# The SSM matrix C loaded and multiplied later in a two-layer decoder kernel, and a first scale with norm weight and bias inside its sums

## What is computed

```python
cs = silu(c)
mod = cs @ ada_w[i] + ada_b[i]                  # 2048 x 12288 per layer
sh1, sc1, g1, sh2, sc2, g2 = split(mod, 6)
h = rms_norm(x, norm1_g[i]) * (1.0 + sc1) + sh1  # the "first scale" is norm1_g * (1 + sc1)
...
# S5: discretisation, per group and state
step = exp(log_step); mag = exp(lr * step); ang = li * step
lb = mag * (cos(ang) + i sin(ang))               # its powers make tables
coef = (lb - 1) / (lr + i li)
bb = coef * b                                    # used here as b, with coef moved into C
y = Re(C x_t)
```

## Time and profile before

| | |
|---|---|
| median of 3 runs | 2718.32 us (2717.66 to 2719.12) |
| the profiled execution, its own time | 2721.41 us |
| its span in the trace | 2719.6 us |
| PE busy | 2653.0 us, 98% |
| VectorE (DVE) busy | 2276.5 us, 84% |
| ScalarE (ACT) busy | 1293.0 us, 48% |
| GpSimd (POOL) busy | 512.4 us, 19% |
| HBM read and written | 701.66 MB and 25.44 MB |

### The profile page before, as it was taken

One profiled execution on the slowest core, in us unless ns is written; L12 is line 12 of the kernel. 1 busy time (PEld: TensorE's weight loads), 2 busy tenths in 40 slices (PEclk: granted clock), 3 DMA queues, 4 the chain that ended last, 5 costly groups with the idle time before them and its releaser, 6 DMA issues.

```text
span 2719.6 us, 50038 instructions
## 1 busy us (share of the span) xinstructions
PE 2653.0 (98%) x18416; PEld 2377.3 (87%) x18416; DVE 2276.5 (84%) x3379; ACT 1293.0 (48%) x1869; POOL 512.4 (19%) x468
## 2 busy tenths in 40 slices
PE   5999999999999999999999999999999999999998
PEld 1998888888898888888888999999888888888887
DVE  6978988888889998899998988998898975677754
ACT  2444444444434655435555344444365553455543
POOL 4142201101133111000101321244411110011122
PEclk8999999999999999999999999999999999999999
DMA  9979989888876987678888968879777765655563
GB/s 377 394 254 346 339 313 344 315 318 321 317 236 219 317 285 256 203 246 307 282 284 269 375 230 250 240 250 328 256 248 250 263 182 188 200 187 190 183 191 117
DMA packets 242267, 725.47 MB, mean 267 GB/s; under 512 B 51106, under 2 KB 60066, under 8 KB 241186
## 3 DMA queue, kind: packets, MB, share of 16 engines
q1 hardware_dynamic: 185184, 666.46, 70.8%
q10 hardware_dynamic: 56900, 56.54, 6.5%
HBM read 701.66 MB, written 25.44 MB: 267 GB/s over the span
## 4 chain that ended last, share of the span: by engine, by line
PE 85%; DVE 2%; POOL 2%; issue 1%; DMA 1%; ACT 0%; ACTq 0%; POOLq 0%; DVEq 0%
PE proj L1929 28%; PE proj L1956 15%; PE proj L1936 14%; PE proj L1959 8%; PE proj L1979 5%; PE proj L1981 4%; PE proj L1980 4%; PE proj L1974 2%; PE proj L1961 1%; PE proj L1977 1%; PE ps L2102 1%; PE ps L2192 1%; DVE w_lo L1202 0%; POOL work L1785 0%; POOL work L1787 0%
## 5 line engine op out<-in xcount | busy, mean ns | idle before, releaser
L606 ACT ACTIVATE w_hi<-raw 128x1024 fp32r<-128x1024 f32 (+1 forms) x896 | 929.7, 1043 | 1118.0 <-PE proj L1936 350.8
L1202 DVE TENSOR_TENSOR w_lo<-raw,w_hi 128x1024 fp32r<-128x1024 f32 (+1 forms) x896 | 1109.9, 1244 | 352.1 <-ACT w_hi L606 341.6
L1929 PE MATMUL proj<-h_hl,w_hi 128*128 128x512 f32 x2656 | 633.7, 391 | 1.7 <-DVE x L1532 1.7
L1929 PEld LDWEIGHTS proj<-h_hl,w_hi 128*128 128x128 f32 x2656 | 488.5, 188 | 97.0 <-DVE x L1532 2.1
L1092 DVE SCALAR_TENSOR_TENSOR ada<-ada,held 128x1024 f32<-128x1024 f32 x304 | 392.5, 1291 | 0.0
L1956 PE MATMUL proj<-h_hl,w_hi 128*128 128x512 f32 x1500 | 381.0, 394 | 0.9 <-DVE work L1388 0.9
L1936 PEld LDWEIGHTS proj<-h_hl,w_lo 128*128 128x128 f32 x2656 | 340.5, 191 | 12.9
L1936 PE MATMUL proj<-h_hl,w_lo 128*128 128x256 f32 x2656 | 344.5, 283 | 0.0
L1835 POOL TENSOR_TENSOR a_hl<-work,a_hl 128x256 fp32r<-128x256 f32 (+1 forms) x88 | 119.6, 1359 | 1135.0 <-ACT a_hl L896 1135.0
L1956 PEld LDWEIGHTS proj<-h_hl,w_hi 128*128 128x128 f32 x1500 | 272.9, 189 | 51.6 <-DVE work L1388 1.2
L1979 PE MATMUL proj<-a_hl,w_hi 128*128 128x256 f32 x864 | 245.7, 284 | 0.8 <-DVE a_hl L1423 0.6
(11 more groups left out here) (287 smaller groups left out, 3369.6 us busy)
## 6 DMA issues: line engine op xcount, KB each, us to landing
raw<-in_w_up SPq DMA_DIRECT2D x352, 512.0 KB, 5.0
ada<-in_ada_t SPq DMA_DIRECT2D x304, 512.0 KB, 5.6
raw<-in_w_in SPq DMA_DIRECT2D x224, 512.0 KB, 6.4
raw<-in_w_down SPq DMA_DIRECT2D x128, 448.0 KB, 4.2
raw<-in_w_down SPq DMA_DIRECT2D x64, 512.0 KB, 3.7
ada<-in_ada_w SPq DMA_DIRECT2D x48, 512.0 KB, 9.1
raw<-in_w_out SPq DMA_DIRECT2D x32, 512.0 KB, 5.0
raw<-in_ssm_w_in SPq DMA_DIRECT2D x32, 512.0 KB, 4.9
```

What stands on the lines that cost most here:

```text
L606: nc.scalar.activation(w_hi[:, j % LAG, 0:nk * P], raw[:, j % s.ring, 0:nk * P], ACT.Copy).then_inc(hi_ready, 1)
L1202: V.tensor_tensor(w_lo[:, j % LAG, 0:nk * P], raw[:, j % s.ring, 0:nk * P], w_hi[:, j % LAG, 0:nk * P].bitcast(F32), ALU.subtract).then_in ...
L1929: mm(proj[b % 2][:, :], w_hi[:, j % LAG, (k - k0) * P:(k - k0 + 1) * P], hl[:, k].rearrange("p c t -> p (c t)"), start=(k == 0), stop=False)
```

## The change

C is no longer loaded in the head, but by ScalarE's queue at step 24 of `qkv0` (the constants are 9 now). GpSimd makes the doublings and both halves of the table first and multiplies C behind them, once C has landed and both early sums are folded (`early_summed` 2); `t16a` and `t16b` lie in the activations' region, so both waits on `prep_done` for `raw` go. The store of C moves from step 14 to step 20 of `qkv1`, where it stands in front of the fourth table store. VectorE makes `gain_diag` (mask times norm weight) and `bias_diag` (mask times 1 + bias) in the head; PE adds `bias_diag` into the scale's sums before piece 26 with four matmuls by the identity; VectorE's `take_scale` then needs a product and a reduction. GpSimd starts on `coef_made`, which now comes with the last squaring of `mag`, and waits for the sum of squares before the table, whose region held the squares.

```diff
--- before.py
+++ after.py
@@ -294,8 +294,10 @@
         t4b, o = cut(a_flat, o, TILES, 4)
         prep, o = cut(a_flat, o, 14, TILES)
         acc_spare = raw[:, RAW - 1, :]
-        t16a, _ = cut(raw_flat, (RAW - 1) * MODW, TILES, SC)
-        t16b, _ = cut(raw_flat, (RAW - 2) * MODW, TILES, SC)
+        t16a, o = cut(a_flat, 0, TILES, SC)
+        t16b, _ = cut(a_flat, o, TILES, SC)
+        bias_diag, o = cut(a_flat, 5 * T, MODB, 32)
+        gain_diag, _ = cut(a_flat, o, MODB, 32)
         early = [cut(h_flat, (KT + 4 * n) * T, MODW)[0] for n in range(4)]
         early += [cut(a_flat, 0, MODW)[0]] + [ada[:, n, :] for n in range(ADA)]
         partial = [cut(work, o, T)[0] for o in (3584, 3840, 4096, 4352, 4608, 4864, 3072, 5120, 5376, 2048, 2304, 2560,
@@ -524,7 +526,6 @@
                     n = s.number(i, j)
                     if name == "qkv0" and j < s.ring:
                         sp.wait_ge(ada_summed, 2 * KT)
-                        wait(sp, prep_done, j // 6)
                     ahead = s.tight if isinstance(i, int) and i == 0 and j < s.ring else s.ring
                     wait(sp, lo_ready, n - ahead + 1)
                     sp.dma_start(raw[:, j % s.ring, 0:nk * P], src(i, blk)[:, k0 * P:(k0 + nk) * P]).then_inc(
@@ -590,13 +591,12 @@
                              (gains, a["gains"]), (slopes, a["slopes"]), (own, a["own"]),
                              (not_first, a["not_first"]), (dskip, a["ssm_d"]), (lane, a["lane"])):
                 act.dma_start(dst[:], src).then_inc(consts_in, 16)
-            act.dma_start(c_raw, a["ssm_c"]).then_inc(consts_in, 16)
             act.wait_ge(row_made, 1)
             act.dma_start(cs_d.unsqueeze(0), cs_first[0:1]).then_inc(row_stored, 16)
             act.wait_ge(x_in, 16)
             for k in range(KT):
                 nc.scalar.activation(squares[:, k, :], x[:, k, :], ACT.Square).then_inc(first_sq, 1)
-            act.wait_ge(consts_in, 16 * 10)
+            act.wait_ge(consts_in, 16 * 9)
 
             def high(s):
                 def f(i, j):
@@ -678,6 +678,10 @@
                     act.dma_start(ef_d.rearrange("n p (k f) -> p k n f", k=4)[:, k],
                                   ef[:, k].rearrange("p (n q) r b -> p n (q r b)", q=4)).then_inc(ef_out, 16)
                 return f
+
+            def load_c_raw(i):
+
+                act.dma_start(c_raw, a["ssm_c"]).then_inc(consts_in, 16)
 
             def store_cw(i):
 
@@ -743,10 +747,11 @@
             s = st["qkv0"]
             late = {b + 4: [hold(b)] for b in range(28)}
             late[28].append(second_half)
+            late[24].append(load_c_raw)
             carry = run_steps(act, s.count, s.length, high(s), late, done=2, keep=True)
 
             s = st["qkv1"]
-            late = {1: [store_lam], 8: [load_rel], 14: [store_cw], 22: [spread_lam(0)], 26: [spread_lam(1)]}
+            late = {1: [store_lam], 8: [load_rel], 20: [store_cw], 22: [spread_lam(0)], 26: [spread_lam(1)]}
             for k in range(4):
                 late.setdefault(17 + k, []).append(store_ef(k))
             for head in range(4):
@@ -1155,25 +1160,32 @@
                 tile_low(number, mod_layer, shift, k0 + nk - 2)
                 tile_low(number, mod_layer, shift, k0 + nk - 1)
 
-            def take_first(q):
-
-                part = FIRST_PARTS[q]
-                cols = slice(part * MODB, (part + 1) * MODB)
-                dve.wait_ge(ada_summed, KT * (q + 1))
-                V.tensor_tensor(diag, first_ps[q], lane[:].unsqueeze(1).broadcast_to([P, MODB, 32]), ALU.mult
+            def take_first():
+
+                cols = slice(0, MODB)
+                dve.wait_ge(ada_summed, KT)
+                V.tensor_tensor(diag, first_ps[0], lane[:].unsqueeze(1).broadcast_to([P, MODB, 32]), ALU.mult
                                 ).then_inc(first_link, 1)
-                dve.wait_ge(first_link, 2 * q + 1)
+                dve.wait_ge(first_link, 3)
                 V.tensor_reduce(mod[:, 0, cols], diag, AX.X, ALU.add).then_inc(first_link, 1)
-                dve.wait_ge(first_link, 2 * q + 2)
+                dve.wait_ge(first_link, 4)
                 V.tensor_tensor(mod[:, 0, cols], mod[:, 0, cols], mod_b[:, 0, cols], ALU.add).then_inc(mod_ready, 1)
 
-            def first_scale(half):
-
-                ks = slice(half * KT // 2, (half + 1) * KT // 2)
-                dve.wait_ge(mod_ready, 2 * half + 2)
+            def take_scale():
+
+                dve.wait_ge(ada_summed, 2 * KT)
+                V.tensor_tensor(diag, first_ps[1], gain_diag, ALU.mult).then_inc(mod_ready, 1)
+                dve.wait_ge(mod_ready, 2)
+                V.tensor_reduce(hscale[:, 0:MODB], diag, AX.X, ALU.add).then_inc(scale_made, 1)
+                dve.wait_ge(scale_made, 2)
+
+            def second_scale():
+
+                ks = slice(KT // 2, KT)
+                dve.wait_ge(mod_ready, 4)
                 V.scalar_tensor_tensor(out=hscale[:, ks], in0=mod[:, 0, KT:2 * KT][:, ks], scalar=1.0,
                                        in1=gains[:, 0, ks], op0=ALU.add, op1=ALU.mult).then_inc(scale_made, 1)
-                dve.wait_ge(scale_made, half + 1)
+                dve.wait_ge(scale_made, 3)
 
             def take_fifth(i):
 
@@ -1203,8 +1215,6 @@
                                     w_hi[:, j % LAG, 0:nk * P].bitcast(F32), ALU.subtract).then_inc(lo_ready, 1)
                     if s.old and isinstance(i, int) and j in s.old:
                         k = s.old[j]
-                        if k == 0:
-                            dve.wait_ge(prep_done, 1)
                         dve.wait_ge(ada_in[k % ADA], 16 * (5 + k // ADA + 1))
                         add_piece(acc_spare, k % ADA, k, k)
                     for m in s.rows_at(i, j):
@@ -1311,20 +1321,25 @@
             link(V.tensor_tensor(m3, m1, bi, ALU.mult))
             link(V.tensor_tensor(m4, m2, br, ALU.mult))
             V.tensor_tensor(lam[:, :, 0, :, 1], four(m3), four(m4), ALU.add).then_inc(lam_made, 1)
-            for _ in range(2):
-                link(V.tensor_tensor(mag[:], mag[:], mag[:], ALU.mult))
+            link(V.tensor_tensor(mag[:], mag[:], mag[:], ALU.mult))
+            V.tensor_tensor(mag[:], mag[:], mag[:], ALU.mult).then_inc(coef_made, 1)
 
             dve.wait_ge(first_sq, KT)
             V.tensor_reduce(sumsq[:], squares.rearrange("p k t -> p t k"), AX.X, ALU.add).then_inc(first_sum, 1)
             dve.wait_ge(first_sum, 1)
-            dve.wait_ge(consts_in, 16 * 10)
-            V.tensor_copy(hscale[:], gains[:, 0, :]).then_inc(coef_made, 1)
-            take_first(0)
+            dve.wait_ge(consts_in, 16 * 9)
+            V.tensor_scalar(hscale[:, 0:MODB], mod_b[:, 0, KT:KT + MODB], 1.0, None, ALU.add).then_inc(scale_made, 1)
+            dve.wait_ge(scale_made, 1)
+            spread = lambda v: v.unsqueeze(2).broadcast_to([P, MODB, 32])
+            V.tensor_tensor(gain_diag, lane[:].unsqueeze(1).broadcast_to([P, MODB, 32]), spread(gains[:, 0, 0:MODB]), ALU.mult
+                            ).then_inc(first_link, 1)
+            V.tensor_tensor(bias_diag, lane[:].unsqueeze(1).broadcast_to([P, MODB, 32]), spread(hscale[:, 0:MODB]), ALU.mult
+                            ).then_inc(first_link, 1)
+            take_first()
             inverse_root(0)
             low(st["qkv0"])(0, 0)
             low(st["qkv0"])(0, 1)
-            take_first(1)
-            first_scale(0)
+            take_scale()
             tiles(0, 0, 0, 0, 8)
 
             def early_adds(j):
@@ -1337,7 +1352,7 @@
 
                 take_early(0)
                 take_early(1)
-                first_scale(1)
+                second_scale()
                 dve.wait_ge(norm_lo, 8)
                 for k in range(8, KT):
                     tile_full(0, k)
@@ -1355,7 +1370,7 @@
                 inverse_root(number)
                 dve.wait_ge(root_ready, number + 1)
                 low(st[following])(0, LO_FIRST - 1)
-                dve.wait_ge(scale_made, number + 2)
+                dve.wait_ge(scale_made, number + 3)
                 tiles(number, mod_layer, shift, 0, KT)
 
             def last_norm():
@@ -1742,15 +1757,9 @@
                 link(G.tensor_tensor(pr, m1, m2, ALU.subtract))
 
             pool.wait_ge(coef_made, 1)
-            cr, ci = c_raw[:, :, 0, :], c_raw[:, :, 1, :]
-            link(G.tensor_tensor(t16a, cr, wide(ncim, SC), ALU.mult))
-            link(G.tensor_tensor(t16b, ci, wide(cim, SC), ALU.mult))
-            link(G.tensor_tensor(cr, cr, wide(cre, SC), ALU.mult))
-            link(G.tensor_tensor(cr, cr, t16b, ALU.subtract))
-            link(G.tensor_tensor(ci, ci, wide(ncre, SC), ALU.mult))
-            G.tensor_tensor(ci, ci, t16a, ALU.add).then_inc(prep_done, 1)
             double(cos, sin)
             double(pr, pi)
+            pool.wait_ge(first_sum, 1)
             e_re, e_im = ef[:, 0, :, 0, :], ef[:, 0, :, 1, :]
             for re, im in ((e_re, e_im), (ef[:, 2, :, 0, :], ef[:, 3, :, 0, :])):
```

(16 more changed lines are left out.)

## The result

| | median, us | runs | ratio to the kernel before, 95% |
|---|---|---|---|
| before, in the same measurement | 2718.80 | 8 | |
| after | 2728.15 (2723.88 to 2730.25) | 8 | 1.0029 (1.0018 to 1.0039) |
| after, measured once more | 2725.51 (2721.61 to 2728.77) | 11 | 1.0020 (1.0011 to 1.0030) |

The change makes the kernel slower, by 9.3 us in one measurement and by 6.0 in the other (before: 2719.49 there). I forecast 2719.2 with a range of 2714.5 to 2723.6, so the time lies outside the range, and above the 0.2% at which I had put a chance of 0.11. The two traces therefore differ by only 2.5 us in all. They show where time goes; how much it comes to in a typical execution is for the medians.

The account below looks back on a forecast made before the run. PE was taken as the bound (busy 98% of the span), with DMA full up to 130 us and around 200 us. Terms -2.6 + 0.8 + 2.7 = +0.9 gave a median of 2719.2 us, range 2714.5 to 2723.6.

Parts of the forecast that it names:

- The C load leaves the head: Up to 130 us, where DMA is full: the stream ends a megabyte earlier, -2.6 us, bounds -1.5 and -4.4.
- The forecast marks: Signs in the profile after: last piece of the first scale near 56.4 not 58.99, PE's step at 130 us about 2.6 earlier.
- Rival 4: Head: freeing of slots, not bytes, paces the last pieces, so the load gives 0; 2721.8 us, chance 0.08.
- the stop of 1.82 for a split: Head, at 79.02 us: PE stood 1.82 us for a w_lo; possible extra gain, not counted in the sum.
- Rival 2: Head gives more: PE's 1.82 us stop at 79.02 goes too and the store is free; 2713.9 us, chance 0.08.
- The small edits: Head: added matmuls, VectorE's small operations, POOL's doublings and dropped waits were all to cost or give 0.
- The C products: Behind the table, about 185 to 197.5 us: POOL slows VectorE, one split reaches PE, +0.8 us.
- The price of a split: VectorE beside POOL: a split took 2.00 us against 1.21 alone, so 0.79 each.
- upper bound of 3.6: VectorE beside the products: four or five slowed splits in 12.5 us would cost at most 3.6 us.
- Only the split beside the first softmax: VectorE beside the products: just this split lacked idle time before the join PE needs, so one was charged, +0.8.
- that rule's result (+3.7): Shared GpSimd and VectorE way into SBUF: all four or five splits pay, 3.6 not 0.8, making the sum +3.7.
- The C store: ScalarE, step 20 between third and fourth table stores: held 3.4 us less 0.7 slack, +2.7, bounds -1.5 and +7.1.
- Rival 3: Weights share the engines with the C store, ScalarE is held 7.77 us, store costs +7.1; 2723.6 us, chance 0.14.

Follow-up runs that it names:

- load_early: The kernel after with the load of C back in the head as the tenth constant, all else as changed; ratio 1.0034 to the kernel before.
- before_spread: The kernel before with only its stores spread over separate steps, C still loaded and multiplied in the head; ratio 0.9998.
- spread_stores: The kernel after with the six products between the two halves of the power table and the five large stores set some steps apart; 2716.37 us, ratio 0.9986.
- old_scale: The kernel after without its edit of the first scale, which is made by the old four operations; ratio 1.0023 to the kernel before.
- no_products: The kernel after without GpSimd's six C products: a buffer is filled instead and the unscaled C is stored; ratio 1.0011 to the kernel before.
- before_store20: The kernel before with one edit, the store of C at step 20 in place of 14; ratio 1.0014, 3.7 us slower.
- products_first_store14: The kernel after with the six products before the table's second half and the store of C back at step 14; ratio 1.0008 to the kernel before.
- products_first: The kernel after with the six products before the table's second half, the store of C still at step 20; 2724.49 us, ratio 1.0019.
- mid_store14: The kernel after with the products straight behind the norm's second half, C's store at step 14 and the table stores at 18 to 21; ratio 0.9998.
- after_again: The kernel after, unchanged, measured and traced a second time; ratio 1.0020 to the kernel before.

## Why the prediction was wrong

**The C load leaves the head, -2.6: right.** The first matmul of the stream comes 3.2 us earlier in the traces, 2.2 of it by load_early's from the load; the medians give 2.2 (before_spread to spread_stores) and, less surely, 2.4 (load_early). By the first scores the traces make it 3.9 (a mean of 187.8 for the four, 183.9 for six of the eight, without the two that have the products in front). The forecast marks were 56.4 for the last piece and an earlier step at 130 us; the piece stood at 54.83, and at 55.7 in the mean of the eight. Rival 4 has fallen. What the head gained beyond the load may belong to GpSimd's order: from 60 to 112 us it is idle, where it was busy for 17.25 us, the stop of 1.82 for a split has become two of 0.29 and 0.61, and the granted clock is 0.96 in place of 0.85. But the DMA share is 1.02 in both, and by the first scores load_early, which has that order without the late load, is 1.8 ahead of the mean of four traces that lie 2.5 apart themselves. So this part isn't told from scatter. Rival 2 as a whole didn't come, since the store wasn't free.

**The small edits, 0: right**, by old_scale.

**The C products, +0.8: this step failed.** They cost 5.8 us, by three traces with the products there (28.16, 28.15, 28.15; a fourth, old_scale, has 26.96) and by no_products (22.34): 4.1 in two stops for VectorE's join and 1.7 in matmuls at the lower clock behind them. The step went wrong in four places.
- The price of a split was read at 0.79 from a row beside the copies of 512 elements. Beside these products it is 1.4.
- I counted only splits. The prediction's upper bound of 3.6 left out VectorE's additions of old pieces, although the section on the kernel says that they run from step 10 on: two of them lost 1.7 and 2.1 us.
- "Only the split beside the first softmax has no idle VectorE time behind it" was read from a schedule that the change itself alters. In the trace of before the idle gaps from 187 to 194 us are 0.36, 0.65 and 1.55, 2.6 in all. The load added is 1.4 + 1.4 + 1.7 + 2.1 = 6.6, on top of the softmax's 0.9 (line 1423 took 1.04 in place of 0.17); less the gaps that is 4.9, of which PE shows 4.1 as stops.
- The sum had no term for the clock. PE's granted clock was 1.00 up to the second stop and 0.50 behind it, and that was worth 1.7.

The products' own length was taken at 12.5 us from the head, where VectorE was partly free; it is 17.0, so they are slowed as well. The Trainium skill ("GPSIMD Engine Reference", 1. Specifications) says that GpSimd shares its way into SBUF with VectorE and that the latter's instructions with two SBUF inputs contend. The trace agrees, and more strongly than I used it: both forms with two inputs double or more, while the softmax's two reductions (lines 1420 and 1421), with one input, take 0.55 and 0.94 in both kernels. I had put that rule's result (+3.7) aside on the ground that not all of the delay reaches PE. With no idle time behind it, most of it does (4.1 of 4.9); and with the low price of a split and no additions, +3.7 was too low as well.

**The C store, +2.7: right in size, in part by luck**, 2.5 by four traces against six, and 3.7 and 3.1 by the medians of the two pairs (before and before_store20, products_first_store14 and products_first). On ScalarE's side the mechanism held. The issue of the fourth store took 2.43 in the first trace of the kernel after, but 3.5 to 3.8 in the six others with C's store at step 20, as forecast; the w_hi behind it came 2.8 us later against the third store (12.98 in place of 10.15). How the holds divide was not foreseen: in the first trace 7.25 was C's own, and the third's fell from 7.77 to 2.55. In all seven traces C's issue alone holds ScalarE for 2.9 to 7.25, but the issues from the third table store to the fourth together for 11.0 to 13.4, against 8.9 to 10.1 in the four with C's store at step 14. What counts is the sum. On PE's side the forecast was 2.7 of waiting; the traces show 1.2 of it, and another 1.1 is the lower clock, which the sum didn't have. Rival 3 asked for a hold of 7.77 on top of the others; one of about that size came, and took the place of the third's, so its price of 7.1 was wrong.

**Sum.** -2.6 + 5.8 + 2.5 = +5.7, against +6.0 in the second measurement and +9.3 in the first; with the 3.9 of the traces for the head it would be +4.4. The remaining 3.6 of the first isn't explained: the two measurements of one kernel differ by 2.6, and no trace shows a place for it. The two traces of the kernel after can't show it, since they are only 1.9 and 1.6 behind the two of before at the third scores: they have the earliest first scores of all (182.52 and 183.25).

## What to carry to other kernels

Before work is put on GpSimd beside VectorE, list every VectorE instruction in that stretch that reads two tiles, give each the slowdown that the same shapes show, and compare the total with VectorE's idle time there. In these runs the six products were free where VectorE had that time (50.1 us up to the first scores in mid_store14 and spread_stores, as in the kernel before), and where it had none, 4.1 of 4.9 us reached PE. Then add what the lower clock behind the stops may cost, 1.7 here. Large stores that one queue issues in a row hold the issuing engine; the same stores some steps apart took 0.4 us of it each. A moved step may be right in one part (the load) and wrong in another (where the arithmetic goes), so move them apart and time them apart.

## What the runs showed of the hardware

- Contention between GpSimd and VectorE in float32 at 128x1024: VectorE's difference of two tiles 1.21 to 2.4 to 2.6 us, with a scalar as third operand 1.27 to 3.0 to 3.4, GpSimd's 1.93 to 2.8 to 3.3. Beside GpSimd's copies of 512 elements the first two take 1.7 to 2.0 and 2.1.
- A store of 2048 packets is accepted in 0.37 us on an empty queue. The third to fifth in a row took 1.9 to 8.3, and which one is held longest changes from trace to trace, while the stretch of the same order of stores changes by some 2 us (26.2 to 28.6).
- PE's granted clock was 0.50 from 198 to 201 us, behind stops of 1.52 and 2.29 us, though PE was full there; the windows of 10 us show it only as 0.89 and 0.94. Matmuls of 256 columns then start 0.21 us apart in place of 0.12. In the stretch with the stores such a run of 12 to 18 matmuls stands behind a stop in six of the seven traces with C's store at step 20 and in none of the other six. after_again, without it, stopped for 0.41 and 1.96 us, and load_early, with it, for 0.44 and 1.96: what decides isn't told here.
